# Four more up projections ahead of the one-hot rounds, and the gates' exponential moved forward

## The reference, cut to what matters

```python
q = (hf @ wq).reshape(T, PEER_HEADS, 2, PEER_DKEY // 2)
sc = einsum('thpd,pnd->thpn', q, subkeys)           # 128 scores for each half key
top_v, top_i = lax.top_k(sc, PEER_TOPK)             # 16 of 128, twice for each head
cand_v = top_v[:, :, 0, :, None] + top_v[:, :, 1, None, :]
best_v, best_j = lax.top_k(cand_v, PEER_TOPK)       # 16 of their pairs
ids = take_along_axis(cand_id, best_j)              # first key * 128 + second key
gates = softmax(best_v)                             # exp, sum, divide
a = einsum('td,ted->te', xb, take(u_tab, ids))      # up projection
w = gates * gelu(a)
y = einsum('te,ted->td', w, take(v_tab, ids))       # down projection
```

## Time and profile before

| | |
|---|---|
| median of the runs | 1405.53 us |
| the profiled execution's own time | 1403.09 us |
| its span, first to last instruction | 1401.3 us |
| PE busy | 1314.0 us (94%) |
| DVE / ACT / POOL busy | 997.7 / 760.5 / 372.7 us |
| mean granted TensorE clock | 0.969 of full |

### The profile page before, as it was taken

One profiled execution on the slowest core, in us unless ns is written; L12 is line 12 of the kernel. 1 busy time (PEld: TensorE's weight loads), 2 busy tenths in 40 slices (PEclk: granted clock), 3 DMA queues, 4 the chain that ended last, 5 costly groups with the idle time before them and its releaser, 6 DMA issues.

```text
span 1401.3 us, 26798 instructions
## 1 busy us (share of the span) xinstructions
PE 1314.0 (94%) x8582; PEld 1184.8 (85%) x8582; DVE 997.7 (71%) x1847; ACT 760.5 (54%) x1260; POOL 372.7 (27%) x252
## 2 busy tenths in 40 slices
PE   6999998997789888998999999999999999999996
PEld 6999998887689788998999967777888888888885
DVE  6799988884567686797788845555666666666666
ACT  6344453554445545545988844444555555555553
POOL 1089812112231024786777700000000000000000
PEclk9999999998899889998999999999999999999998
DMA  9877784442365533453333345555756556565561
GB/s 337 316 247 263 242 271 164 141 151 79 130 196 186 175 106 136 160 178 127 110 118 111 116 151 180 180 180 180 240 184 192 191 181 189 188 192 181 192 188 67
DMA packets 68024, 249.21 MB, mean 178 GB/s; under 512 B 7808, under 2 KB 8192, under 8 KB 67200
## 3 DMA queue, kind: packets, MB, share of 16 engines
q1 hardware_dynamic: 58896, 214.80, 46.5%
q10 hardware_dynamic: 9072, 33.69, 7.1%
HBM read 245.83 MB, written 2.62 MB: 177 GB/s over the span
## 4 chain that ended last, share of the span: by engine, by line
PE 81%; DVE 9%; ACT 4%; issue 3%; DMA 2%; POOL 1%; ACTq 0%; DVEq 0%; SPq 0%; POOLq 0%
PE ps L1567 30%; PE ps L1953 26%; PE ps L1967 10%; PE ps L1969 5%; PE ps L1934 4%; ACT pr L511 2%; PE ps L1706 1%; DVE small L1000 1%; DVE s L995 1%; PE ps L1842 1%; DMA ada<-adaT 1%; DVE WL L799 1%; PE ps L1716 1%; DMA raw<-stream 1%; PE ps L1694 1%
## 5 line engine op out<-in xcount | busy, mean ns | idle before, releaser
L799 DVE TENSOR_TENSOR WL<-raw,WH 128x1024 fp32r<-128x1024 f32 x326 | 412.3, 1268 | 174.7 <-ACT WH L397 171.6
L397 ACT ACTIVATE WH<-raw 128x1024 fp32r<-128x1024 f32 x394 | 414.4, 1055 | 178.1 <-PE ps L1953 85.3
L1567 PE MATMUL ps<-X,WH 128*128 128x256 f32 x1840 | 347.3, 290 | 6.1 <-DVE X2L L919 4.1
L1567 PEld LDWEIGHTS ps<-X,WH 128*128 128x128 f32 x1840 | 292.1, 196 | 7.3 <-DVE X2L L919 4.3
L1567 PE MATMUL ps<-X,WL 128*128 128x256 f32 x920 | 263.5, 286 | 0.0
L1967 PE MATMUL ps<-X,WH 128*128 128x512 f32 x608 | 216.9, 397 | 0.0
L1953 PE MATMUL ps<-WH,wvH 128*128 128x512 f32 x512 | 207.5, 405 | 2.6 <-DVE wvL L1337 2.4
L1953 PE MATMUL ps<-WH,wvL 128*128 128x512 f32 x512 | 202.5, 396 | 0.0
L1953 PE MATMUL ps<-WL,wvH 128*128 128x512 f32 x512 | 202.0, 395 | 0.0
L1539 POOL TENSOR_TENSOR WL<-raw,WH 128x1024 fp32r<-128x1024 f32 x68 | 164.0, 2413 | 82.5 <-ACT WH L397 82.5
L1567 PEld LDWEIGHTS ps<-X,WL 128*128 128x128 f32 x920 | 179.1, 195 | 0.0
(11 more groups left out here) (262 smaller groups left out, 2185.6 us busy)
## 6 DMA issues: line engine op xcount, KB each, us to landing
raw<-stream SPq DMA_DIRECT2D x394, 512.0 KB, 3.4
ada<-adaT ACTq DMA_DIRECT2D x48, 512.0 KB, 4.2
bias<-att_bias ACTq DMA_DIRECT2D x9, 512.0 KB, 4.5
x<-xT SPq DMA_DIRECT2D x2, 512.0 KB, 6.7
ws<-wsT SPq DMA_DIRECT2D x1, 1024.0 KB, 11.6
lng<-rows SPq DMA_DIRECT2D x1, 1024.0 KB, 8.1
lnb<-rows SPq DMA_DIRECT2D x1, 1024.0 KB, 7.1
bsb<-rows SPq DMA_DIRECT2D x1, 1024.0 KB, 8.1
```

What stands on the lines that cost most here:

```text
L397: act.activation(WH[:, slot, :], raw[:, slot, :], ACT.Copy).then_inc(h_done, 1)
L799: dve.tensor_tensor(WL[:, slot, :], raw[:, slot, :], WH[:, slot, :].bitcast(F32), ALU.subtract).then_inc(l_done, 1)
L1567: mm = pe.matmul(out_ap, a(kc), b(kc), start=(first and kc == 0 and i == 0), stop=(last and kc == KC - 1 and i == 2))
```

## The change

TOP becomes 24, so EARLY becomes 56 and LATE 72: four of the up projections that had stood in the late stage now run ahead of the rounds, and four down projections move from the late stage to the row of early ones. The tile `below` begins at 24 KB of the shared area instead of 20. The last of the 24 early up projections, u(23), stands on PE behind the transposes of the lists, and its gelu on ACT behind the first `hot_second`. The exponential stands on ACT behind the sixteenth gelu instead of behind the last one.

```diff
-TOP = 20
+TOP = 24
 EARLY = TOP + T // 8
@@ ScalarE
+            def early_gelu(j, g=None):
+                act.wait_ge(chunk_done, up(C_U + j + 1, g, 4))
+                act.activation(tiles(A, j, g, 4), ps[:, j % 2:j % 2 + 1, 0:T], ACT.Gelu).then_inc(gelu_ready, 1)
+
             def early_step(j, g=None):
                 hi(C_U + 3 + j, g)
-                act.wait_ge(chunk_done, up(C_U + j + 1, g, 4))
-                act.activation(tiles(A, j, g, 4), ps[:, j % 2:j % 2 + 1, 0:T], ACT.Gelu).then_inc(gelu_ready, 1)
+                early_gelu(j, g)
                 if g is None and j == 0:
                     sc_out(2 * PH - 1)
-            fours(act, TOP, early_step)
+            fours(act, TOP - 8, early_step)
             act.wait_ge(exp_in, 1)
             act.activation(best[:, :, :], best[:, :, :], ACT.Exp).then_inc(exp_ready, 1)
+            for j in range(TOP - 8, TOP - 1):
+                early_step(j)
+            hi(C_U + 3 + TOP - 1)
             act.wait_ge(lt_mm, 1)
             act.activation(tmp[2][:, :], i2_l, ACT.Copy).then_inc(lt_ready, 1)
...
             hot_second(0)
+            early_gelu(TOP - 1)
             for e in range(ROUNDS):
@@ TensorE
-            fours(pe, TOP, early_up)
+            fours(pe, TOP - 4, early_up)
+            for j in range(TOP - 4, TOP - 1):
+                early_up(j)
             pe.wait_ge(lists_ready, 1)
...
             mm.then_inc(lt_mm, 1)
-
+            early_up(TOP - 1)
```

## The result

The changed kernel took 1396.2 us, the median of 4 executions (1395.47 to 1397.01), against 1405.82 us for the kernel before, the median of 4 (1404.94 to 1407.23). The ratio is 0.9931, 95% interval 0.9914 to 0.9948. The forecast was 1398.9 us with a range of 1396.4 to 1402.2: the direction was right, the measured 9.6 us were more than the forecast 6.65, and the time lies 0.2 us under the range. The profiled execution took 1395.47 us, 7.6 less than the one of before. Its span is 1393.7 us and its mean granted clock 0.975, against 0.969.

The account below looks back on a forecast made before the run. TensorE, busy 94% of the span, was taken as the bound. +3.94 (round 0 later) - 22.35 (late pairs) + 11.76 (early down) = -6.65 off 1405.53 gave 1398.9 us; range 1396.4 to 1402.2.

Parts of the forecast that it names:

- The exponential behind the sixteenth gelu: On ScalarE, table load, exponential and reload fit into idle time; gelu 16 ends at 640.8, 0.8 slack, no cost.
- Rival 3: ScalarE's table switches cost more than their loads and hold u(18) up by 1.8: -4.85 us, 1400.7; chance 0.06.
- The lists at 647.7: With the exponential ready early, VectorE completes the lists at 646.45 + 1.22 = 647.7, before the transposes need them.
- Three up projections and the transposes: On TensorE, u(20) to u(22) run to 656.00, then the transposes at once and at full clock to 656.67.
- The chain under u(23): Lists to round 0: POOL's low part delays the Relu, TensorE stands about 1.65, round 0 ends 3.94 us later.
- Rival 2: Round 0's second half waits less for POOL: 1397.6; with u(23) covering everything -8.65 us, 1396.9, chance 0.15.
- The clock behind them: TensorE's clock stays full behind round 0's pauses of 0.4 and 1.65: nothing taken, 1.85 us kept for the range.
- Rival 1: The clock falls behind round 0's pauses, costing 1.85 us: -4.8 in all, 1400.7; chance 0.27.
- Rounds 1 to 31: Each round stays at 4.66 us, bound by TensorE; VectorE grows by at most 0.09 a round; no cost.
- rival 4: VectorE becomes the bound of the rounds, growing by 0.65 a round: +3.3 us, 1408.8; chance 0.02.
- Four fewer late pairs: In the late stage, four pairs at 5.587 us each disappear: 22.35 us saved.
- Four more early down projections: In the early down projections behind the rounds, four more at 2.94 us each: 11.76 us added.

Follow-up runs that it names:

- the second profile of before: The kernel before, unedited, measured and profiled once more beside itself: 1405.67 us, ratio 1.0012.
- the second and third of the changed kernel: Profiles of the changed kernel, unedited, measured twice more against the kernel before: 1398.12 us, ratio 0.9965, and 1396.96 us, ratio 0.9952.
- the first repeat: The changed kernel, unedited, measured a second time against the kernel before: 1398.12 us over 7 executions, ratio 0.9965.

## Why the prediction was right or wrong

*The exponential behind the sixteenth gelu: right.* Load, exponential, `hi`, reload and gelu stand as forecast; the gelu ended at 641.24 against 640.8, all of the difference from a start that was 0.5 later. u(18) did not wait. There was no time between a table load's end and the next instruction (636.88 + 1.28 = 638.16, then 638.17). Rival 3 is out. *The lists at 647.7: wrong by 1.5, at no cost.* They were ready at 649.7, because of the multiplication of 1.95 us that had to wait for POOL; the transposes come 6.6 us later. I had taken its 0.42 from rows in which POOL was idle.

*Three up projections and the transposes: right.* The transposes began at 656.35, the forecast 656.00 plus the later start.

*The chain under u(23): right, and the point where the forecast was at its best.* Low part at 657.95 (657.52), difference at 660.31 (659.89), square at 661.44 (661.03), second half of round 0 at 662.88 (662.5), its end at 666.91 (666.27). S1 grew by 4.04 and 3.88 in the two pairs, where 3.94 were forecast. The pauses were 0.26 and 1.47. Rival 2 is out with it, though its time with full cover, 1396.9, is the nearest of all to the measured 1396.2: the time alone would have pointed to the wrong mechanism.

*The clock behind them: right.* It stayed at full in round 0 in all three profiles of the changed kernel, here in the first. Rival 1 is out. Why 0.52 and 1.70 ended at half clock in the earlier trace rows and 0.26 and 1.47 did not, no run shows; the choice between the two rows was argued, and came out.

```profile
655.00:668.00 13.00, 11.27 (x95) 10.91 (x94) 7.13 (x12) 8.03 (x13) 10.20 (x6) 1.00 0.41 129
```

*Rounds 1 to 31: right.* The rounds' 4.66 stayed, so rival 4 is out. This window answers to the last of the earlier trace rows; VectorE's busy time grew by 2.69, which is 0.09 a round, the bound of the forecast:

```profile
666.91:811.40 144.49, 144.46 (x1241) 144.26 (x1239) 124.35 (x213) 123.08 (x184) 104.44 (x61) 1.00 0.34 114
```

*Four fewer late pairs: right*, -22.34 for -22.35. *Four more early down projections: right in kind*, +11.9 and +12.1 between the second profile of before and the second and third of the changed kernel, where the clock fell in both kernels. In the first pair of profiles it was +10.21, since there the clock fell behind the rounds in the kernel before (window below) and not in the changed one. The sum had no term for this: 1.55 us of the difference between the two first profiles come from it, and the second and third profile of the changed kernel have it the other way.

```profile
810.40:813.60 3.20, 3.20 (x9) 2.45 (x9) 0.30 (x1) 0.00 (x0) 0.00 (x0) 0.50 0.50 164
```

*The step that failed* is the last one, the range about the median: "The range goes from rival 2's full cover with half a us of the runs' own spread". The sum, -6.65, is what the pooled executions give (-6.68 with a standard error of 0.48, or -6.94 with all executions of the kernel before). But single executions of the kernel before lie between 1400.49 and 1408.71, with a standard deviation of 1.4 to 1.7 us, and a median of three or four of them is off by about 1 us on either side of a comparison (an estimate from these deviations). The first comparison had both the kernel before 1.3 above its pooled mean and the changed one 1.6 below its own. The half us that I allowed for the spread was too little.

Part of the 1.6 goes with the mean clock: it was 0.9742 in those four executions against 0.9725 in all 17, which at 0.66 us for 0.001 (a fit over these 17) is 1.1 us. What sets the clock of an execution ahead of the lists, in the same instructions, stays open. The profiles differ there by up to 14 us of half clock (61.4 to 75.1 up to 600 us), and the first mark lies between 592.0 and 596.4 us without a close tie to it. That the first comparison's interval and that of the first repeat don't overlap is hardly the spread of single executions alone; whether it is the build, the chip or chance was not tested.

## What to carry to other kernels

Work that is merely placed, not added, is sized by cutting the span at marks and comparing stretches: here S1 repeats to 0.15 us and S3, but for one profile, to 0.1, while whole executions swing by 8, so a few profiles cut that way size such a change better than a handful of whole times, and a range for a median of four has to hold that swing beside the sum. When independent work is put under a chain to cover it, look at what comes with it in the queues of the other engines: the conversion that fed the added up projections stood ahead of the very instructions that were to be covered. Moving its two halves away shortened S1 by 1.9 us (221.24 to 219.36), and turning the lists earlier by 0.3 more, of the 8.9 us that full cover would have given (6.68 pooled, and these 2.2). Don't take the duration of a VectorE instruction with two SBUF operands from a stretch in which POOL is idle.

## What the runs showed of the hardware

A VectorE multiplication of 128x256 with both operands in SBUF took 1.89 us instead of 0.42 with POOL at work on SBUF, ended 0.28 behind POOL's instruction, and took 0.42 again with one operand in PSUM. The granted clock after one and the same pause of 2.42 us fell in 11 of 14 profiles, and cost 1.2 to 1.8 us when it did (S2 of kernels with as many up projections ahead). The pauses of 0.26 and 1.47 us in round 0 made it fall in none of three profiles.
